# Sample-attention keys and softmax weights turned by VectorE instead of TensorE, and convolution weights issued from ScalarE's queue

## The reference, cut to what matters

```
for (w, d) in DILATED_PATTERNS:                 # (128,1), (512,4), (2048,16)
    idxs.append(q_idx[:, None] - d * arange(w // d + 1))
kg, vg = k_all[:, idx], v_all[:, idx]
s = einsum('bthc,btkhc->bthk', q, kg) * HEAD_DIM ** -0.5 + bias
p = softmax(where(valid, s, NEG))
out = einsum('bthk,btkhc->bthc', p, vg)
```

## Time and profile before

| | |
|---|---|
| median of three runs | 1083.66 us (1082.96 to 1085.27) |
| the profiled execution | 1082.67 us, span 1080.7 us |
| PE busy | 1036.0 us, 96% of the span |
| DVE busy | 523.0 us, 48% |
| ACT busy | 312.7 us, 29% |
| POOL busy | 212.4 us, 20% |
| mean granted TensorE clock | 0.982 of full speed |

### The profile page before, as it was taken

One profiled execution on the slowest core, in us unless ns is written; L12 is line 12 of the kernel. 1 busy time (PEld: TensorE's weight loads), 2 busy tenths in 40 slices (PEclk: granted clock), 3 DMA queues, 4 the chain that ended last, 5 costly groups with the idle time before them and its releaser, 6 DMA issues.

```text
span 1080.7 us, 15684 instructions
## 1 busy us (share of the span) xinstructions
PE 1036.0 (96%) x5834; PEld 620.1 (57%) x5834; DVE 523.0 (48%) x1175; ACT 312.7 (29%) x665; POOL 212.4 (20%) x240
## 2 busy tenths in 40 slices
PE   7999999999999999999999999989999999889997
PEld 6888875565878777766555554334433333345443
DVE  6836634777733464545556464441111110047674
ACT  2332313777533322301111123111111111244331
POOL 0100001121433352531012111322231110130000
PEclk9999999999999999999999998989999999989999
DMA  9713214940563666663973237989999999974321
GB/s 315 190 31 116 71 50 119 293 101 6 215 213 112 212 211 216 207 244 81 355 270 128 94 105 280 405 340 414 418 410 410 419 420 399 371 288 157 119 78 78
DMA packets 99260, 242.11 MB, mean 224 GB/s; under 512 B 21206, under 2 KB 56958, under 8 KB 84528
## 3 DMA queue, kind: packets, MB, share of 16 engines
q1 hardware_dynamic: 88544, 212.10, 54.1%
q0 software_dynamic: 9920, 26.38, 6.4%
q10 hardware_dynamic: 720, 2.62, 0.6%
HBM read 210.12 MB, written 35.65 MB: 227 GB/s over the span
## 4 chain that ended last, share of the span: by engine, by line
PE 80%; DVE 6%; DMA 6%; SPq 4%; issue 2%; ACT 2%; POOL 0%; POOLq 0%; DVEq 0%; ACTq 0%
PE pair L2921 13%; PE pair L3124 13%; PE pair L2598 10%; PE pair L2976 9%; PE pair L3146 6%; PE pair L3228 5%; PE pair L3223 3%; PE pair L2739 2%; DMA h_dram<-R 2%; DMA R<-in_w_up 2%; PE pair L2713 2%; PE pair L3047 2%; PE pair L2755 2%; PE pair L3111 1%; SPq L707 1%
## 5 line engine op out<-in xcount | busy, mean ns | idle before, releaser
L2921 PE MATMUL pair<-R 128*128 128x264 f32 x672 | 160.2, 389 | 0.2 <-POOL R L1032 0.2
L3124 PE MATMUL pair<-R 128*32 128x512 f32 (+2 forms) x896 | 151.3, 601 | 5.2 <-DMA R<-in_w_up 3.0
L2598 PE MATMUL pair<-R 128*128 128x256 f32 x672 | 149.7, 382 | 0.4 <-DVE R L1755 0.4
L2598 PEld LDWEIGHTS pair<-R 128*128 128x128 f32 x672 | 127.0, 191 | 18.8 <-issue 1.0
L2921 PEld LDWEIGHTS pair<-R 128*128 128x128 f32 x672 | 123.5, 190 | 23.4 <-issue 3.5
L2976 PE MATMUL pair<-R 128*128 128x512 f32 x256 | 116.6, 606 | 0.0
L2329 DVE TENSOR_TENSOR R<-pair,R 128x256 f32<-128x256 f32 x21 | 8.9, 425 | 208.3 <-ACT R L1516 208.3
L3124 PEld LDWEIGHTS pair<-R 128*32 128x32 f32 (+2 forms) x896 | 48.8, 125 | 92.2 <-issue 87.8
L3146 PE MATMUL pair<-R,bias 128*32 128x512 f32 (+2 forms) x448 | 78.0, 611 | 2.7 <-issue 2.1
L2976 PEld LDWEIGHTS pair<-R 128*128 128x128 f32 x256 | 47.7, 192 | 53.3 <-issue 52.6
L3228 PE MATMUL pair<-R 128*128 128x512 f32 x168 | 73.0, 593 | 0.0
(11 more groups left out here) (366 smaller groups left out, 1471.5 us busy)
## 6 DMA issues: line engine op xcount, KB each, us to landing
R<-in_w_gate SPq DMA_DIRECT2D x32, 1024.0 KB, 12.3
R<-in_w_up SPq DMA_DIRECT2D x32, 1024.0 KB, 15.6
R<-in_w_down SPq DMA_DIRECT2D x32, 1024.0 KB, 16.8
R<-in_w_in SPq DMA_DIRECT2D x12, 1024.0 KB, 8.4
R<-in_x_prompt SPq DMA_DIRECT2D x16, 512.0 KB, 3.8
R<-in_cache_k SPq DMA_DIRECT2D x8, 1024.0 KB, 5.0
R<-in_cache_v SPq DMA_DIRECT2D x8, 1024.0 KB, 4.9
R<-y_dram SPq DMA_DIRECT2D x16, 512.0 KB, 5.9
```

What stands on the lines that cost most here:

```text
L2598: last = mm(qbank(p, part, k), lhs[:, c, :], rhs[:, c, :], start=(c == 0), stop=(c == 3))
L2921: last = mm(cbank(n, k), lhs[:, c, :], rhs[:, c, :], start=(c == 0), stop=(c == 3))
L3124: last = mm(bk[2 + u][r, :].rearrange("p (w f) -> p w f", w=2), xgT[u][:, c, r], wgu[s][:, :, c, :], start=(c == 0), stop=(c == DC - 1))
```

## The change

Keys: a `key` part is now two DVE instructions that turn 32x32 blocks from the ring straight into `kT`; PE and ACT have no part in it. Within blocks of 32 cache rows the turned keys come out as 16 tiles of [128 rows, 224 columns], the four 32-row groups of a tile holding 32 of a head's 64 values for 32 consecutive rows of each of seven chunks, so that a sample's 896 scores now lie in four rows of 224 (`PART`) instead of one of 896.

Scores: 16 matmuls of 256 columns (224 and 32 for the new tokens) a sample, four side by side. Two samples instead of four make a pass (`NPASS` is 4), so `soft`, `norm` and `turn` run four times. Greatest score and sum must be joined over the four rows of a query: `by_group` does it with small turns and reductions on DVE.

Weights: PE multiplies the two samples' weights with a permutation matrix (`regroup`, one matmul of 512 columns), and DVE turns the result in 32x32 blocks into `PTs` (a new part, `put`). Order and weights of the parts change, and `ITEMS` with them.

Loads: ACT issues the convolution weights of set n + 1 behind its copy of the first product of set n; SP's queue holds ring items only.

Small edits: 16 DVE copies of the samples' queries at steps 9 to 24 of the prompt's attention; the samples' q and k are turned by 32 small matmuls instead of 8 transposes; the bias is added in quarters; `relbd` takes eight DMAs of a quarter of the elements, behind the first two stores of turned inputs, and DVE spreads the table further.

```diff
-        def keys(b, gg):
-            slot, arrived = item("k", b)
-            kv = KV[slot]
-            pe.wait_ge(S(f"ring_in{slot}"), arrived)
...
-            for r in range(4):
-                last = pe.transpose(bk[4][:, P * r:P * r + P], kv[:, r, P * gg:P * gg + P], ident[:, :])
...
+        def turn_keys(b, gg):
+            slot, arrived = item("k", b)
+            kv = KV[slot]
+            if gg == 0:
+                dve.wait_ge(S(f"ring_in{slot}"), arrived)
+                if b >= 1:
+                    dve.wait_ge(S("ss_done"), b)
...
+            dve.transpose(out[:, 0:4], raw[:, 0:4])
+            dve.transpose(out[:, 4:7], raw[:, 4:7]).then_inc(S("kt_done"), 1)
+
+        def by_group(cols, op, src, group, out):
+            then(dve.transpose(cols, src))
+            then(dve.tensor_reduce(group, cols.rearrange("p (h i t) -> p h t i", h=2, i=4), AX.X, op))
+            if op == ALU.add:
+                then(dve.reciprocal(group, group))
+            return dve.transpose(out.rearrange("p (h i t) -> p h i t", h=2, i=4),
+                                 group.rearrange("p (h t) -> p h t", h=2).unsqueeze(2).broadcast_to([P, 2, 4, NT]))
...
+            for s in range(2):
+                then(dve.tensor_tensor_reduce(Es[:, s, :], bk[6 + g % 2][:, ROW * s:ROW * s + ROW], bias_s, -1.0, 3e38, ALU.add, ALU.min,
+                                              least[:, s:s + 1]))
+                if 2 * g + s + 1 < NB:
+                    new_bias(2 * g + s + 1)
+            by_group(least_t, ALU.min, least, group_least, nms).then_inc(S("ss_scored"), 1)
+            for b in (2 * g + 2, 2 * g + 3):
+                if b < NB:
+                    spread_q(b)
...
+            then(by_group(dens_t, ALU.add, dens, group_den, rdens))
+            for s in range(2):
+                dve.tensor_scalar(Es[:, s, :], Es[:, s, :], rdens[:, s:s + 1], None, ALU.mult).then_inc(S("ps_ready"), 1)
...
+            dve.transpose(PTs.rearrange("p s c x -> p (s c x)"), bk[4]).then_inc(S("st_done"), 1)
...
+            for hh in range(2):
+                for half in range(2):
+                    for j in range(NG):
+                        n = 4 * j + 2 * hh + half
+                        at = 32 * n + (0 if hh else 16)
+                        last = mm(out[strips[j], ROW * second:ROW * second + ROW], qbd_all[second][:, at:at + 32], kT[:, n, :],
+                                  start=(second == 0 and hh == 0 and half == 0), stop=(second == 1 and hh == 1 and half == 1))
...
+            mm(bk[4], regroup, Es.rearrange("p s n -> p (s n)"), start=True, stop=True).then_inc(S("st_full"), 1)
...
+        def load_conv(n):
+            act.wait_ge(S("cv_full"), PRODUCTS * (n - 1))
+            act.dma_start(wC[n % 2], conv_weights(n)).then_inc(S(f"w_in{5 + n % 2}"), 16)
...
+        parts += [*keys[0][0:2], ("norm", g - 1), *keys[0][2:3], ("turn", g - 1), *keys[0][3:4], ("put", g - 1)]
+        if g < NPASS:
+            parts += [("score", 2 * g)]
+        parts += [("weigh", b), *keys[1][0:2], ("sum", b), ("weigh", b + 1), *keys[1][2:4]]
+        if g < NPASS:
+            parts += [("score", 2 * g + 1), ("soft", g)]
+        parts += [("sum", b + 1)]
...
+ROOM = {"key": 4, "score": 6, "soft": 2, "norm": 2, "turn": 2, "put": 2, "weigh": 8, "sum": 4}
```

More of the change, by code:

```diff
@@ L97, in constants @@
     c["c_log_p"] = np.tile(log_count(dist)[None, :], (H, 1))
[L99 to L103, removed]
+    chunk, r = np.arange(PART) // 32, np.arange(PART) % 32
+    first = np.where(chunk < 4, PAST - NEAR + 4 * r + chunk, 512 * (chunk - 4) + 16 * (r // 4) + r % 4)
     t = np.arange(NT)
-    cache_dist = PAST + t[:, None] - row[None, :]
@@ L112, in constants @@
[L112 to L117, removed]
-    r = np.arange(P)
-    c["c_mask"] = (2 * (r[:, None] % 32 // 8) + r[:, None] % 2 == np.arange(AD)[None, :] // DH).astype(np.float32)
-    c["c_sel"] = (r[:, None] % 8 // 2 == np.arange(NT)[None, :]).astype(np.float32)
+    c["c_hot_s"] = hot.reshape(P, SKN).astype(np.float32)
@@ new lines, in constants @@
+    r = np.arange(P)
+    quarter, token = r % 16 // NT, r % NT
+    log = np.full((P, PART + SAMP + NB * SAMP), NEG, np.float32)
+    for i in range(4):
+        log[quarter == i, 0:PART] = log_count(dist[i])[token[quarter == i]]
+    for b in range(NB):
+        own = (np.arange(SAMP)[None, :] // NT == b) & (quarter[:, None] == 0)
+        log[:, PART + SAMP + SAMP * b:PART + 2 * SAMP + SAMP * b] = np.where(own, log_count(new_dist)[token], NEG)
+    c["c_log_s"] = log
+    row_at = 32 * quarter + 8 * (r // 32) + 4 * (r % 32 // 16) + token
@@ L197 @@
[L197 to L206, removed]
@@ L207, with sample_order @@
-ROOM = {"key": 4, "score": 4, "turn": 6, "weigh": 8, "sum": 4}
+    return i % 3, sum(ARRIVES[k] for k, _ in ITEMS[i % 3:i + 1:3])
+RING_USED = tuple(sum(ARRIVES[k] for k, _ in ITEMS[s::3]) for s in range(3))
+def sample_order():
+    parts = []
+    for g in range(NPASS + 1):
+        keys = [[("key", 2 * g + d, gg) for gg in range(NG)] if g < NPASS else [] for d in range(2)]
+        if g == 0:
+            parts += keys[0] + [("score", 0)] + keys[1] + [("score", 1), ("soft", 0)]
+            continue
+        b = 2 * g - 2
+        parts += [*keys[0][0:2], ("norm", g - 1), *keys[0][2:3], ("turn", g - 1), *keys[0][3:4], ("put", g - 1)]
[5 more added lines that the diff above has]
+        parts += [("sum", b + 1)]
+    return parts
@@ L224, with place_of @@
 PARTS_AT = spread_parts()
-def place_of(kind, b, gg=None):
-    return next(s for s, parts in PARTS_AT.items() for part in parts if part[0:2] == (kind, b) and (gg is None or part[2] == gg))
+def place_of(part):
+    return next(s for s, parts in PARTS_AT.items() if part in parts)
 NSTAT = 6
@@ L490, in _build @@
     PTf = view(R1, 20480, 2, 6, P)
[L492 to L498, removed]
+    kT = view(R1, 15392, 16, ROW)
+    Es = view(R1, 19488, 2, ROW)
+    PTs = view(R1, 20000, 2, 8, 32)
+    qbd = [view(R1, 20512 + 512 * s, 16, 32) for s in range(2)]
+    qbd_all = [view(R1, 20512 + 512 * s, 512) for s in range(2)]
+    least, least_t, nms, dens, dens_t, rdens = (view(R1, 21536 + 32 * k, 32) for k in range(6))
+    group_least, group_den = (view(R1, 21728 + 8 * k, 8) for k in range(2))
+    masked = view(R1, 21952, AD)
     sel = view(R1, 22464, NT)
+    mask, regroup = view(R1, 22472, H), view(R1, 22472 + H, P)
     as_raw = view(R4, 5680, CC, SAMP)
@@ L801, in _ @@
             load_item(i)
-        sp.dma_start(mask, I["c_mask"]).then_inc(S("small_in"), 16)
+        sp.dma_start(R1[:, 22472:22472 + H + P], I["c_mask"]).then_inc(S("small_in"), 16)
         sp.dma_start(sel, I["c_sel"]).then_inc(S("small_in"), 16)
[L805 to L814, removed]
+        for i in range(3, len(ITEMS)):
+            load_item(i)
         sp.wait_ge(S("so_full"), 6)
@@ L2096, in sample_part @@
         def sample_part(kind, b, *more):
-            if "norm" in more:
-                normalise_sample(0 if kind == "key" else 1)
+            if kind == "key":
+                turn_keys(b, more[0])
+            if kind == "soft":
+                score_sample(b)
+            if kind == "norm":
+                normalise_sample(b)
+            if kind == "put":
+                put_ps(b)
             if kind == "weigh":
                 mask_sample(b)
-            if "soft" in more:
-                score_sample(b // 4)
-            if kind == "score" and b == 3:
-                spread_q(1)
-                new_bias(1)
             if kind == "sum":
                 keep_sum(b)
-            if "sum" in more:
-                keep_sum(more[-1])
         dve.wait_ge(S("late_in"), 16 * NLATE)
@@ L2888, in sample_part @@
         def sample_part(kind, *more):
-            if kind == "key":
-                keys(more[0], more[1])
             if kind == "score":
```

283 lines of the change are left out of this document (131 added, 152 removed).

## The result

The changed kernel takes 1087.61 us (median of 12 runs, 1084.32 to 1092.28), the kernel before 1083.41 us in 12 runs beside it: a ratio of 1.0045, 95% interval 1.0029 to 1.0060. It is slower by a little under half a per cent, where I forecast it faster by as much.

The account below looks back on a forecast made before the run. PE in the convolution stage was taken as the bound. Stage -5.9, q and k matmuls +1.3, query copies +1, start -0.8 gave -4.4 us against the 1083.66 median: 1079 us, eight in ten 1067 to 1097.

Parts of the forecast that it names:

- PE's own work: Convolution stage: 32 key parts leave PE, scores and regrouping cost more; with one old wait gone, 22.4 us shorter before new waits.
- DVE's prices: Convolution stage: a key part's two turns cost DVE 1.1 us (ends 0.97 and 1.6); DVE busy 160 us in all.
- Rival 2: DVE's key turns become the bound: no gain from 1.27 us a part, 1092 at 1.6, 1108 at twice the price; chance 0.24.
- scores 0 and 1: First two scores in the convolution stage: DVE falls behind over eight key parts, so PE waits 2.3 us.
- the turns behind 19, 38, 57 and 73: PE's regrouping of weights behind these convolution products waits for DVE: 2.6, 0, 1.4 and 2.8 us.
- the last `put`: End of the convolution stage: PE has one product left while DVE must join it and turn the weights; 2.7 us wait.
- the other scores and the one weighing: Six scores and one `weigh`, each behind two to four key parts: PE waits 0.45 us each, 3.1 together.
- New waits: Convolution stage: PE's waits at scores, turns, `put`, ACT's copies and convolution weights sum to 16.5 us, leaving 5.9 gained.
- The weights on ACT: Convolution weights issued by ACT: nothing to win; one set of twelve lands late, about 1.1 us lost, bounds 0 to 6.
- Outside the stage: Small q and k matmuls +1.3 us, query copies in the prompt's attention +1, DVE's idleness at the start -0.8.
- DVE keeps up: Rival 1, convolution stage: PE stays the bound with a third of the waits, 5.5 us; 1068 us; chance 0.14.
- That nothing is gained: Rival 4: PE's key turns only filled time it would have waited for joins anyway; 1083 us; chance 0.08.

Follow-up runs that it names:

- The version without waits: Changed kernel with the same work, parts laid on other products, and some DVE work at the convolution stage's start moved behind products 5 and 7: 1061.32 us, ratio 0.9807.

## Why the prediction was wrong, step by step

- **PE's own work: right.** I had 22.4 us less, 0.9 of it a wait, so 21.5 of work. The version without waits shows 194.81 against 217.04: 22.2.
- **DVE's prices: right.** A turn of 512 elements takes 0.698 us, one of 384 0.533; neighbours overlap, and the steps of the chain are 0.62 and 0.46, 1.08 for a part where I had 1.1. DVE is busy for 158.65 us where I had 160. The Trainium skill's figure ("VectorE: DVE Perf Modes", The three transpose paths: 311 ns for 128x128, given there for bf16), from which I had worked out an estimate of 2.2 us, does not hold for these float32 instructions. Rival 2 falls by its price, though the time landed between its 1083 and its 1092: that the sign came out as that rival had it is no support for it.
- **Where PE waits: right; how long: 3.6 us short.** In the order of the prediction, forecast and measured from PE's timeline: scores 0 and 1, 2.3 and 2.85; the turns behind 19, 38, 57 and 73, 2.6 and 3.88, 0 and 0, 1.4 and 2.01, 2.8 and 3.38; the last `put`, 2.7 and 2.20; the other scores and the one weighing, 3.1 and 3.51; ACT's copies, 0.5 and 0; the convolution weights, 1.1 and 0.4. Unforeseen were 1.83 us at the stage's start, where I had the clearings and the query spreads at 0 behind a cover that was not there. Together 16.5 and 20.1. At the first turn I had priced `norm` at its undisturbed 1.35 us and the two joins at 0.9; POOL's sums ran beside them, the joins took 1.83 together and the two scalings alone 1.33:

```profile
327.72 1.83 DVE L1957 TENSOR_TENSOR R<-R 128x264 f32<-128x264 f32 x2
...
330.44 1.33 DVE L2114 TENSOR_SCALAR R<-R 128x256 f32<-128x256 f32 x2
```

- **The step that failed: "New waits: ... = 16.5 us. The stage gains 22.4 - 16.5 = 5.9."** It prices a wait at its length. Three of them came with a granted clock of 0.50, 4.8 us in all by the windows, and PE's work around the waits took some 2.5 more (202.08 - 194.81 = 7.3 together). For most of the 2.5 there is an estimate: the modelled end of the matmul in front of a wait counts as busy and nothing covers it, 0.16 us (two products in a row are busy for 3.83 us and the next work starts after 3.67), and 14 waits make 2.2. Put together: 22.2 less work, 1.1 of old waits less, 20.1 of waits and 7.3 of slower work more, 4.1 us longer, as measured. From the forecast's 5.9 us shorter that is 10.0 away: 4.8 by the clock, 3.6 by longer waits, 2.5 by the work around them, less 0.9 won elsewhere. With the clock priced, 1.1 us of the stage's 5.9 would have been left, and no gain of the kernel could have been forecast. The Trainium skill ("TensorE: Matmul & The Clock Gate", HAM oscillation — how this bites in real kernels) warns of this, for gaps that DMAs make: a gap in TensorE's work puts its clock back to half, and the work behind the gap pays. The trace agrees, 0.50 behind waits of 3.88, 3.38 and 2.20 us, though not behind that of 2.01. That rule spoke against this change, and I looked for one at the DMA queues instead.
- **The weights on ACT: small, as I had it, but not for my reason.** PE lost 0.4 us to POOL where I had 1.1. But the move isn't neutral: undone alone it costs 5 us, in the profile most of it low clock; with spread parts it is worth nothing. The Trainium skill's rule that I had cited ("DMA: Bandwidth & Descriptors", Issuing engines are not separate DMA queues) was not what decided. The trace agrees with it where the parts are spread, with a median of 5.9 us to landing from either queue; in the places of the change it is 7.5 us from ACT and 8.6 from SP.
- **Outside the stage: right in sum, 1.4 against 1.5, by luck.** The prompt's attention starts 1.1 us earlier (183.3 for 184.4; forecast 0.8) and takes 2.1 longer (forecast 2.3). But the small matmuls of q and k took 0.68 us where the old turns took 0.61, so 0.1 more and not 1.3, and the 2.1 is elsewhere. Some 0.8 of it is lost by 197.3 us, ahead of the first query copy at 216.5, where a low clock lasted longer (0.79 on the mean from 184 to 200 us, 0.89 before). Behind that PE is idle for 4.5 us instead of 3.4, waiting for DVE's scalings, where the query copies lie. Neither was tried in a run.
- **Rivals.** DVE keeps up (1068) was false of this table of places and nearly true of the next: 1063.8 with the same instructions. That nothing is gained was not so either: the work did leave PE.

Not tried: the old turning of the weights with the new keys, and the prompt's attention without the query copies.

## What to carry to other kernels

Work that moves from a full engine to a half-empty one is worth its length only if the places on the second engine are laid anew: count, at each place where the full engine needs a result, the products between the last thing that the other engine can do and the need, and put single pieces where that engine now idles. Price a wait of TensorE not by its length alone but with the stretch at half clock that may follow it; three waits cost 4.8 us extra here. When an undoing "costs" time, see first whether it only moved a disturbance onto a chain that had no slack, and whether the cost is wait or clock.

## What the runs showed of the hardware

- Beside POOL's sums, DVE's operations on SBUF took two to four times as long (scaling of 256 elements 0.35 us alone, up to 0.88 beside POOL; a copy of 32 columns 0.18 and 0.71), but not its turns: all 32 of the 512-element ones lie between 0.657 and 0.712 us, one at 383.39 us with POOL's sums beside it at 0.70.

```profile
L2085 DVE STREAM_TRANSPOSE R<-R x32: 657/703/712, 296.8 to 460.4; 128x512 f32<-128x512 f32 x32
```

- A matmul of identity by identity, 128 columns of float32, took 0.23 us in a row, a transpose of the same size on the same engine 0.11 in the earlier trace rows's key parts (seven in 0.77 us). I had priced the one by the other.
- A granted clock of 0.98 over a stage, beside 1.00 before, hid 4.8 us; the mean of a long window doesn't show that it was three stretches of 3 us at 0.50.
- The length of a wait alone did not decide what came behind it: one of 3.88 us was followed by 3.4 us of work at half clock, one of 3.91 us by 5.8 (weights back on SP's queue), and 2.95 us at the same turn with fewer turns by none.
